# Softplus by two heads instead of four, three modulation dots moved, and a pair of launch matmuls reordered, in a two-model kernel on one core

## The reference

```python
def ada_mod(c, w, b):
    m = jax.nn.silu(c) @ w + b          # 1024 -> 6 * 1024: shift, scale, gate, twice
def modulate(h, shift, scale):
    return h * (1 + scale) + shift
```

```python
log_1mb = where(strict, log_sigmoid(-z), 0)      # z = q k^T / 8
after   = reverse_cumsum(log_1mb) - log_1mb
a       = where(strict, exp(log_sigmoid(z) + after), 0)
```

## Time and profile before

| | |
|---|---|
| time, three runs | 1487.48, 1490.86 and 1503.12 us, median 1490.86 |
| the profiled execution: its own time, and its span | 1496.56 us, 1494.7 us |
| mean granted TensorE clock | 0.995 |
| busy: PE, DVE, ACT, POOL | 1465.0 us (98%), 1038.9 us (70%), 852.9 us (57%), 85.6 us (6%) |
| the attention stage's share of the span | about 42 to 150 us |

### The profile page before, as it was taken

One profiled execution on the slowest core, in us unless ns is written; L12 is line 12 of the kernel. 1 busy time (PEld: TensorE's weight loads), 2 busy tenths in 40 slices (PEclk: granted clock), 3 DMA queues, 4 the chain that ended last, 5 costly groups with the idle time before them and its releaser, 6 DMA issues.

```text
span 1494.7 us, 30216 instructions
## 1 busy us (share of the span) xinstructions
PE 1465.0 (98%) x11600; PEld 1380.3 (92%) x11600; DVE 1038.9 (70%) x1833; ACT 852.9 (57%) x1452; POOL 85.6 (6%) x136
## 2 busy tenths in 40 slices
PE   8998999999999999999999999999999999999999
PEld 6777999999989999999998989889999898989999
DVE  2887777799687666555675857886676684787664
ACT  4445555544555745656566765564556676655553
POOL 0110000011000000000020000220000000021000
PEclk9999999999999999999999999999999999999999
DMA  9865588899575455666663545236666355423663
GB/s 362 326 226 172 170 290 278 283 335 355 191 259 194 127 175 165 196 195 188 195 229 118 173 155 159 98 100 184 199 196 213 106 171 169 148 92 113 187 198 124
DMA packets 81183, 292.02 MB, mean 195 GB/s; under 512 B 9185, under 2 KB 10465, under 8 KB 80946
## 3 DMA queue, kind: packets, MB, share of 16 engines
q1 hardware_dynamic: 68274, 244.31, 50.7%
q0 software_dynamic: 11792, 42.77, 8.5%
q10 hardware_dynamic: 1008, 3.41, 0.6%
HBM read 289.40 MB, written 1.05 MB: 194 GB/s over the span
## 4 chain that ended last, share of the span: by engine, by line
PE 90%; DVE 5%; ACT 3%; issue 2%; DMA 0%; SPq 0%; DVEq 0%; ACTq 0%
PE G L495 22%; PE G L497 22%; PE G L496 22%; PE G L554 2%; PE G L556 2%; PE G L555 2%; DVE wlo L1547 2%; PE O L1038 1%; PE S L1007 1%; PE Tp L963 1%; PE G L576 1%; PE Tp L891 1%; DVE aw L1555 1%; ACT whi L1092 1%; PE G L582 1%
## 5 line engine op out<-in xcount | busy, mean ns | idle before, releaser
L1547 DVE TENSOR_TENSOR wlo<-raw,whi 128x1024 fp32r<-128x1024 f32 x444 | 548.4, 1237 | 283.2 <-ACT whi L1092 280.5
L1092 ACT ACTIVATE whi<-raw 128x1024 fp32r<-128x1024 f32 x444 | 468.8, 1058 | 233.7 <-PE G L497 180.0
L495 PE MATMUL G<-h,whi 128*128 128x256 f32 x2096 | 596.9, 285 | 1.1 <-DVE at L2127 0.7
L497 PE MATMUL G<-h,wlo 128*128 128x256 f32 x2096 | 582.1, 278 | 0.0
L496 PE MATMUL G<-h,whi 128*128 128x256 f32 x2096 | 582.1, 278 | 0.0
L495 PEld LDWEIGHTS G<-h,whi 128*128 128x128 f32 x2096 | 394.1, 188 | 9.6 <-issue 5.9
L496 PEld LDWEIGHTS G<-h,whi 128*128 128x128 f32 x2096 | 394.2, 188 | 1.8 <-issue 0.5
L497 PEld LDWEIGHTS G<-h,wlo 128*128 128x128 f32 x2096 | 395.1, 188 | 0.0
L1555 DVE CUSTOM_DVE_ANT_0 aw<-aw,cs,cols 128x1024 f32<-128x1024 f32 x80 | 102.2, 1277 | 0.0
L495 PE MATMUL G<-ah,whi 128*128 128x256 f32 x352 | 98.0, 278 | 0.0
L496 PE MATMUL G<-ah,whi 128*128 128x256 f32 x352 | 98.0, 278 | 0.0
(11 more groups left out here) (341 smaller groups left out, 2268.4 us busy)
## 6 DMA issues: line engine op xcount, KB each, us to landing
raw<-in_w SPq DMA_DIRECT2D x444, 512.0 KB, 3.7
aw<-in_ada POOLq DMA_DIRECT2D x80, 512.0 KB, 5.4
adaw<-in_ada SPq DMA_DIRECT2D x8, 1024.0 KB, 15.6
sn<-in_uq ACTq DMA_DIRECT2D x2, 768.0 KB, 4.2
x<-in_x SPq DMA_DIRECT2D x1, 1024.0 KB, 5.3
pt<-in_ukv ACTq DMA_DIRECT2D x2, 512.0 KB, 5.4
out<-x SPq DMA_DIRECT2D x4, 256.0 KB, 2.3
dec<-in_dec ACTq DMA_DIRECT2D x1, 512.0 KB, 4.3
```

The source lines that it names most:

```text
L495: pe.matmul(o, wh, mv[:, 0:T], start=(k == 0), stop=False)
L497: ins = pe.matmul(o, wl, mv[:, 0:T], start=False, stop=(k == k_of - 1))
L1092: act.activation(whi[:, s, :], raw[:, s, :], ACT.Copy).then_inc(w_hi, 1)
L1547: dve.tensor_tensor(wlo[:, s, :], raw[:, s, :], whi[:, s, :], ALU.subtract).then_inc(w_lo, 1)
```

## The change

- `softplus_part` and `softplus` take two heads at a time, in four parts: ACT's at b = 16, 18, 20, 22 instead of two at 18, 22, and DVE's at b = 17, 19, 21, 23 instead of two at 19, 23. `sb_sums(hh)` waits for part hh // 2.
- The dots after b = 8, 10 and 11 are gone. Their order stays, so every later dot moves up in the list: b = 23 now has two, one comes after the last `o_split`, and the output projection runs three (21, 22, 23) instead of two (22, 23).
- In the launch `ada_rows(1, 1)` runs before tile 3's first half instead of behind it, and the `keep_busy(2)` behind it is gone.

```diff
-ATT_DOTS = [b for b in range(1, 25) if b not in (5, 9)]
+ATT_DOTS = sorted([b for b in range(1, 25) if b not in (5, 8, 9, 10, 11)] + [23])
...
             ada_cols(1, 0)
+            ada_rows(1, 1)
             run_first([(k, 3) for k in range(4)])
-            ada_rows(1, 1)
-            keep_busy(2, Tp[:, 0, :])
             ada_cols(1, 1)
             keep_busy(6, Tp[:, 0, :])
...
-                pe.wait_ge(sb_sp, hh // 4 + 1)
+                pe.wait_ge(sb_sp, hh // 2 + 1)
...
-                z4 = zs[:, 4 * g2:4 * g2 + 4, :]
-                s4 = sp[:, 4 * g2:4 * g2 + 4, :]
-                act.wait_ge(s_free, ATT_S.index(f"z{4 * g2 + 3}") + 1)
-                chain.link(act.activation(s4, z4, ACT.Abs))
-                chain.link(act.activation(s4, s4, ACT.Exp, scale=-1.0))
-                act.activation(s4, s4, ACT.Ln, bias=1.0).then_inc(sb_ln, 1)
+                z2 = zs[:, 2 * g2:2 * g2 + 2, :]
+                s2 = sp[:, 2 * g2:2 * g2 + 2, :]
+                act.wait_ge(s_free, ATT_S.index(f"z{2 * g2 + 1}") + 1)
+                chain.link(act.activation(s2, z2, ACT.Abs))
+                chain.link(act.activation(s2, s2, ACT.Exp, scale=-1.0))
+                act.activation(s2, s2, ACT.Ln, bias=1.0).then_inc(sb_ln, 1)
...
-                if b in (18, 22):
-                    softplus_part(b // 4 - 4)
+                if b in (16, 18, 20, 22):
+                    softplus_part(b // 2 - 8)
...
-                dve.scalar_tensor_tensor(out=s4, in0=z4, scalar=0.0, in1=s4, op0=ALU.max, op1=ALU.add).then_inc(sb_sp, 1)
+                dve.scalar_tensor_tensor(out=s2, in0=z2, scalar=0.0, in1=s2, op0=ALU.max, op1=ALU.add).then_inc(sb_sp, 1)
...
-                if b in (19, 23):
-                    softplus(b // 4 - 4)
-                if b in ATT_DOTS:
-                    ada_later(ATT_DOTS.index(b))
+                if b in (17, 19, 21, 23):
+                    softplus(b // 2 - 8)
+                for r, bb in enumerate(ATT_DOTS):
+                    if bb == b:
+                        ada_later(r)
             for p in range(4, 8):
                 o_split(p)
+            ada_later(len(ATT_DOTS))
...
-            x_update(B_ATT_O, 8, G_ATT_O, one_each, 2, 4, later=(22, 23))
+            x_update(B_ATT_O, 8, G_ATT_O, one_each, 2, 4, later=(21, 22, 23))
```

More of the change, by code:

```diff
@@ L1645, in softplus @@
             def softplus(g2):
-                z4, s4 = zs[:, 4 * g2:4 * g2 + 4, :], sp[:, 4 * g2:4 * g2 + 4, :]
+                z2, s2 = zs[:, 2 * g2:2 * g2 + 2, :], sp[:, 2 * g2:2 * g2 + 2, :]
                 dve.wait_ge(sb_ln, g2 + 1)
-                dve.scalar_tensor_tensor(out=s4, in0=z4, scalar=0.0, in1=s4, op0=ALU.max, op1=ALU.add).then_inc(sb_sp, 1)
+                dve.scalar_tensor_tensor(out=s2, in0=z2, scalar=0.0, in1=s2, op0=ALU.max, op1=ALU.add).then_inc(sb_sp, 1)
             def minus_sums(hh):
```

## The result

The changed kernel takes **1483.22 us**, median of 9 runs (1480.3 to 1489.91), against 1495.76, median of 9 runs of the kernel before beside it (1487.48 to 1503.12). The ratio is 0.9949, with a 95% interval of 0.9927 to 0.9971. By this ratio it is 7.6 us less (11 to 4), a real gain and yet within 1%. The ratio isn't the quotient of the two medians: the medians lie 12.5 us apart and the means of the same runs 10.3. The profiled executions: 1489.58 us after (span 1487.6) and 1496.56 before.

A forecast was written before the change was run, and what follows sets the result against it. TensorE, busy in 98% of the span, was taken as the bound. Eight terms summed to -9.1 us, giving 1487.5 from the profiled execution or 1481.8 from the median; 1485 was taken between them, range 1477 to 1494.

The forecast's parts named there:

- Launch: Launch: rows before tile 3's half let the columns start sooner, 0.7 us less (bounds 0 and 0.8).
- Dots: Before the first moba scores and first transposes: three dots of 1.20 us leave DVE's queue, 3.6 us less (2.6 to 3.7).
- rival 2: Weight loads bind once DVE is quicker: of 3.6 us from moved dots only 2.6 or less come, 1486 to 1488.6; chance 0.08.
- Softplus, first part: ACT after the fifth head's exponentials: 0.85 us an instruction, 2.5 a part; later moba scores wait 0.6 us more (0 to 1.5).
- Rival 3: Two heads' activation costs nearly as much as four heads', 1.5 us: slower by 1.9, 1492.8 or 1498.5; chance 0.03.
- Second part: b = 18, last transposes: wait of 2.00 shrinks to 0.1 to 0.4, 1.7 us less; half clock goes, another 1.7 less.
- Third part: First sums: DVE's 0.9 us piece before the first `minus_sums` makes the fourth sum wait, 0.5 us more (0 to 1).
- Fourth part: Last four sums: fifth starts at once, eighth waits 2.0, 0.7 us less; half clock from 140.4 to 144.0 goes, 1.8 less.
- rival 1: The new 2.0 us wait before head 7's sum is followed by half clock, price 1.7 us, so 1486.7; chance 0.22.
- signs of being wrong: Activations of 768 over 1.2 us; clock 0.5 within 110 to 145 us; longer raw-block waits before first transposes; shift lost behind the stage.
- rival 4: The profiled half clock was chance, absent from the median: only the waits' 5.6 us come, 1485.3 or 1491; chance 0.14.

## Why the prediction was right

It was 1485.0 for a measured 1483.22, and a gain of about 9 for a measured 7.6. That the time came out within 2 us is partly luck. The 1485 was a choice between 1481.8 and 1487.5, made because the starting time was so uncertain, and the kernel before, run beside the changed one, had a median of 1495.76 instead of 1490.86: less the 9.1 that is 1486.7, and less the measured 7.6 it is 1488.2. The steps are the better test. They can be laid beside the stage's sections, each the difference to before, in us. "Full clock" is the repeat without half clock (stage 99.02). The wait in front of the fifth sum is counted in the last section. Sums are made before rounding.

| section | predicted | profile after | full clock |
|---|---|---|---|
| launch (rows to columns) | -0.7 | -0.8 | -0.8 |
| stage start to first transposes | -3.6 | -3.3 | -3.6 |
| to last transposes (+0.6, -1.7) | -1.1 | -1.4 | -1.4 |
| to first sum (half clock) | -1.7 | -1.6 | -1.6 |
| first to fifth sum | +0.5 | +0.3 | +0.3 |
| fifth sum to projection (-0.7, -1.8) | -2.5 | -0.6 | -2.1 |
| sum | -9.1 | -7.3 | -9.1 |

- **Launch.** Right, term and mechanism: the columns start 3.33 us behind the rows, 3.40 in the prediction, and the copy was ready.
- **Dots.** Right: 3 x 1.20. The other three profiles of the changed kernel have 3.62, 3.61 and 3.62. The profile shown lacks 0.36, with ACT waiting 10.1 us for `raw` in the stretch from 40 to 75 against 8.8 before and 7.6 in the kernel with the work at b = 22. The repeats have 7.9, 7.4 and 8.3. That fits what rival 2 describes, at a third of its price of 1.0 and in one profile of four, but no run shows it to be the cause. The wait for `mqk`, 0.4 to 1.0 in some of the profiles, with and without the moved dots, wasn't foreseen.
- **Softplus, first part.** Right: 0.83 to 0.84 an instruction for a predicted 0.85, 2.5 a part, and 0.56 of wait for a predicted 0.6. Moving this part one slot later removed the wait, which confirms its cause. Rival 3 (0.85 against 1.5) is excluded by these durations. By the Trainium skill's "VectorE: DVE Perf Modes", section "The TRN2 errata", 224 cycles and 768 at 1.2 GHz, it would be 0.83 us, an estimate: the trace agrees.
- **Second part.** The wait was to shrink to 0.1 to 0.4 and is nothing; the half clock went, as said.
- **Third part.** 0.3 instead of 0.5, a wait of 0.23.
- **Fourth part.** The wait in front of the eighth sum was predicted with its cause (two dots in front of `minus_sums`) at 2.0 and measured 1.67; 0.3 of it is spent before the seventh sum instead. The step that failed is the last one of the sum: "The half clock from 140.4 to 144.0 goes, 1.8 us less, if the new wait of 2.0 brings no other". It brought one in three of four profiles. That was rival 1, priced at 1.7; it cost 1.3 to 1.5. Its chance of 0.22 was too low even by its own argument, "two of four such waits cost nothing", which makes it even odds. Those two lay in the first half of the stage, and the two in the second half, where the new one was to come, had both been followed by half clock. Over all profiles that is nine of ten against one of five; it is a frequency, and the exceptions on both sides show that it is no rule.

Of the signs of being wrong that were named, one came: a clock of 0.5 between 110 and 145 us, at 135.4 to 138.8. ACT's longer wait for raw blocks (10.1 us against 8.8) came in the profile shown and in none of the repeats. The projection starts 8.3 us sooner for "some 9", and 0.9 of that lies ahead of any edit. So the forecast of the time and the mechanism of seven of its eight terms held, each section within 0.4 us in the profile at full clock, and one condition, that no new half clock comes, didn't.

Averaged over the four profiles of the changed kernel, the stage is 100.2, 7.2 less than before, and with the launch 8.0; the runs say 7.6 (11 to 4). So about the whole gain lies in the edited stretch, and rival 4 (the medians see only the waits' 5.6) has nothing for it: in three of three kernels with the old waits the half clock was there. But its 5.6 lies inside the interval of the runs, so it is the profiles that speak against it, not the times.

## What to carry to other kernels

A helper's work that is moved lands in some queue: add up what stands in front of each release there after all the edits together, since three parts worth 10.6 us alone gave 7.3 together, and one dot of 1.2 us in the wrong slot cost about 2.7 with the half clock behind its wait. Where TensorE's wait is near 2 us, count the half clock behind it in. Here it followed 10 of 15 such waits in the stage, nine of ten in its second half, so one profile can't tell whether it will come. And ask whether TensorE waits again right behind it: then it costs nothing, as before the first transposes with the launch edit alone, and otherwise it cost 1.3 to 1.6 us. And compare edits of a few us by stretches of the trace between two instructions that both kernels have; the whole time here moves by 7 us and more for reasons that have nothing to do with the edit.

## What was not expected: two paces at full clock

The stage gained 6.5 us, but the difference between the two profiles runs from 8.3 us (start of the first feed-forward stage: 168.04 against 176.33) up to 14.9 at its end, and back to 6.4 at the end of the second. Each of these stages is a row of 1584 matmuls of 256 columns, with TensorE busy for over 99% of it, at granted clock 1.00, and yet it takes one of two lengths. After:

```profile
168.00:350.20 182.20, 180.66 (x1585) 1.00 0.88 306
...
560.50:748.00 187.50, 187.44 (x1584) 1.00 0.59 182
```

and before, the other way round:

```profile
176.30:365.00 188.70, 187.52 (x1584) 1.00 0.86 295
...
573.80:755.00 181.20, 180.64 (x1584) 1.00 0.61 189
```

It isn't waiting: each matmul is longer. Groups of one line and form in the stretch from 200 to 300 us (busy, mean ns of one, idle), before:

```profile
L495 PE MATMUL G<-h,whi 128*128 128x256 f32 x284 | 79.8, 281 | 0.0
```

after:

```profile
L496 PE MATMUL G<-h,whi 128*128 128x256 f32 x262 | 72.3, 276 | 0.0
```

From start to start, by the timelines, it is 117.8 ns in the one and 113.3 in the other, 4% apart. Over the 13 profiles here (before, after and eleven runs) the first of the two stages took 182.1 to 182.2 us eight times and 188.7 five times, and the second 181.3 eleven times and 188.2 twice; nothing in between. Which it is goes with no edit: the changed kernel's own four profiles have 182.2, 182.1, 182.2 and 188.7 in the first stage. With a price of 6.5 to 6.9 us it would sort the runs of the changed kernel into 1480 to 1483 and 1488 to 1490. The four that have a profile agree: 1480.1 and 1481.1 without a slow stage, 1489.6 and 1489.9 with one. For the others it isn't shown. DMA doesn't go with it: the first stage ran quick with 306 GB/s, the second slow with 182. The output projection shows two lengths too, 25.8 to 25.9 us in seven profiles and 26.7 in five, and the one between, 26.5, is the kernel with five dots there. What sets the pace stays open, and no run here was made for it.
